# Merging the last two down groups and turning x through HBM ahead of the odd mixer

## The chip, the core and the metric

The kernel runs on one core of one Trainium2 chip. The core has a matrix engine (TensorE: PE in the profile, with its weight loads as PEld), a vector engine (VectorE, DVE), a scalar engine (ScalarE, ACT), GpSimd (POOL) and a sync engine (SyncE, SP) that only issues DMAs here. Each engine runs its own program in order, and the programs meet at semaphores. The metric is the device time of one execution in microseconds, lower is better.

## What is computed

Two layers over 256 tokens with 2048 features, all in float32. Each layer is a mixer and a gated convolution FFN, each behind an RMS norm, each added to x. Cut to what matters here:

```python
for i in range(2):
    h = rms_norm(x, norm_mix_g[i])
    if i == 0:   # "even" mixer: spatial gating and windowed pooling
        mix = concat([y_a, y_b]) @ w_out_even
    else:        # "odd" mixer: 16 heads of forgetting attention
        p = h @ w_in_odd          # q, k, v (2048 each) and 16 forget logits
        mix = forgetting_attention(q, k, v, cumsum(log_sigmoid(f + b))) @ w_out_odd
    x = x + mix
    up = rms_norm(x, norm_ffn_g[i]) @ w_up[i]              # 2048 -> 2 * 5632
    x = x + (silu(conv3(gate)) * conv3(val)) @ w_down[i]   # 5632 -> 2048
return rms_norm(x, final_norm_g)
```

## The kernel before

**Pieces.** All weights stream through in 369 pieces of 1 MB. SyncE loads a piece into one of four `raw` slots (`load`, L299), ScalarE rounds it to a high part (`high`, L457), VectorE subtracts to get the low part (`low`, L858), and TensorE multiplies: high weights with the high and the low part of the activations, low weights with the high part. The scalar and the vector program are written out piece by piece: at step k they do the piece that TensorE needs three pieces later (`LEAD = 3`), and other work is put at chosen steps around it. `high` of piece c+3 may begin when TensorE is through piece c-1, since the slot is a ring of four. `load` of a piece waits for the low part of the piece four before it.

**x and h.** x lies as `x[128 tokens, 2 tiles, 2048]`. The matrix products need h with features on partitions, `H[128, 16, 512]` (`h_split`: 256 columns high, 256 low). x is turned in four chunks of 512 features. A chunk is turned either by TensorE (`transpose_x`, 8 products with the identity, L1468) or by VectorE (`turn_blocks`, 16 transposes of 32 partitions, L902); then ScalarE multiplies with the norm's gain and rounds (`turned_high`, L495, four instructions), and VectorE forms the low part (`turned_low`, L882, four instructions). `s_turn` counts turned chunks, `s_turn_hi` their high halves, `s_turned` chunks of h that are ready; for the odd mixer (stage 2) they begin at 8, 16 and 8. The row scale of the norm (`rstd`) is applied later, to the outputs: ScalarE squares x (`squares`, L479), VectorE adds up (`mean_square`, L916), ScalarE takes the root (`root`, L502), VectorE refines it (`rstd_columns`, L921 to L925) and spreads it over a tile (`spread_rstd`, L941).

**The end of the first FFN.** The hidden features go in 11 groups. The last 16 pieces (`B + 116` on) are 8 of the last group's up projection, then 4 of the tenth group's down projection (`down(l, NG - 2)`) and 4 of the eleventh's. Each down piece gives 512 columns of x for one group: 24 products, then `add_to_x` (L911) adds them to x, 8 times in all. With the last four pieces TensorE also turns chunks 0, 1 and 2 of x. Steps 8 to 15 below are these eight pieces.

**The start of the odd mixer** (`heads_of_group(0)`, called M0 to M11 below, one per piece). M0 and M1 are the first half of the v projection, M2 and M3 first halves of q and k; before M4 TensorE does `forget_sums` (16 products, L1698), then the second half of v. VectorE turns chunk 3 in M0, ScalarE and VectorE finish chunk 3 of h at step M2, and VectorE spreads rstd at the end of its step M2. The forget logits pass through ScalarE and VectorE at step 5, then through HBM by GpSimd (`c_rows`) into the bias tile that the first head's logits need at M9.

Of the kernel before, what the change touches and what calls it, by code (L numbers as in the profile page):

```python
# [25 lines left out]
F32 = mybir.dt.float32  # L26
# [23 lines left out]
def build(nc, x_in, norm_mix_g, norm_ffn_g, final_norm_g, w_in_even, ln_v_g, ln_v_b, w_spatial,  # L50
          b_spatial, w_pool, pool_scale, w_out_even, w_in_odd, b_forget, w_out_odd, w_up, conv_w,
          conv_b, w_down, out, c_dram):
# [21 lines left out]
    N_END = N_FFN[1] + 12 * NG  # L74
    OUT0_ORDER = [(c, q) for c in range(4) for q in (2, 3, 0, 1)]
# [8 lines left out]
    A_OUT0, A_FFN, A_OUT1 = 0, [4, 4 + 4 * NG + 4], 4 + 4 * NG  # L84
# [6 lines left out]
    X_READY = [0, A_OUT0, A_FFN[0] + 4 * (NG - 1), A_OUT1, A_FFN[1] + 4 * (NG - 1)]  # L91
# [8 lines left out]
    OUT = out[0].rearrange("(t p) d -> p t d", p=P)  # L100

    with ExitStack() as ctx:
# [67 lines left out]
        xT = [work[:, c0:c0 + 1024].rearrange("p (k t) -> p k t", k=4) for c0 in (0, 1024, 2048, 4096)]  # L170
        scaled = raw[:, 0:2, :]
# [29 lines left out]
        s_turn = sem("x_turned")  # L201
        s_turn_hi = sem("turned_high")
# [75 lines left out]
        def turned_bank(s, n, kk):  # L278


            if s in (1, 3) or (s, n) in ((0, 3), (2, 3)):
                return xT[n if s else 0][:, kk, :]
            return psT[:, 2 * (n % 2) + kk // 2, TOK * (kk % 2):TOK * (kk % 2) + TOK]
# [9 lines left out]
        def _(sp):  # L293
# [43 lines left out]
            def load_ffn(l):  # L337
                B = N_FFN[l]

                def panels(c, g, pair, r=0):  # L340

                    for j, first in enumerate((0, FF)):
                        for k in range(2):
                            col = value(sp, at(512 * g + 256 * pair + first, 512, r))
                            load(c + 2 * j + k, W_UP[l][:, 8 * k:8 * k + 8, bass.ds(col, 256)], r)

                def down(c, g, r=0):
                    row = value(sp, at(4 * g, 4, r))
# [12 lines left out]
                panels(B + 120, NG - 1, 1)  # L361
                down(B + 124, NG - 2)
                down(B + 128, NG - 1)
# [73 lines left out]
        def _(a):  # L437
# [47 lines left out]
            def turned_high(s, n):  # L485
# [5 lines left out]
                for kk in range(4):  # L491
# [5 lines left out]
                    if kk % 2:  # L497
                        fenced(ins, s_turn_hi, 8 * s + 2 * n + kk // 2 + 1)

# [131 lines left out]
            def ffn(l):  # L631
# [40 lines left out]
                for k in range(16):  # L672
                    if k >= 14 and l == 0:
                        turned_high(s + 1, k - 14)
# [30 lines left out]
                    if l == 0 and k >= 13:  # L705
                        squares(s + 1, k - 13)
# [21 lines left out]
            def heads_of_group(first, r=0):  # L728

                c = N_MIX1 + 12 * first  # L730
                for k in range(12):
                    hh = 4 * first
                    if first == 0 and k == 0:
                        turned_high(2, 2)
                        squares(2, 3)
                    if first == 0 and k == 1:
                        root(2)
                    if first == 0 and k == 2:
                        turned_high(2, 3)
                    if first == 0 and k == 5:  # L740
# [97 lines left out]
        def _(ve):  # L838
# [53 lines left out]
            def turn_blocks(s, n, tokens):  # L892
# [10 lines left out]
                if 3 in tokens:  # L903
                    ins.then_inc(s_turn, 1)

# [218 lines left out]
            def ffn(l):  # L1124
# [48 lines left out]
                for k in range(16):  # L1173
                    if k >= 14 and l == 0:
                        turned_low(s + 1, k - 14)
                    low(c + k + LEAD)
                    if k == 0:
# [18 lines left out]
                    if k >= 8 and not (l == 1 and k >= 12):  # L1196
# [50 lines left out]
            def heads_of_group(first, r=0):  # L1247
                c, hh = N_MIX1 + 12 * first, 4 * first
                for k in range(12):
                    if first == 0 and k == 0:  # L1250
                        turned_low(2, 2)
                        turn_blocks(2, 3, (0, 1))
                        mean_square(2)
                        turn_blocks(2, 3, (2, 3))
                    if first == 0 and k == 1:
                        rstd_columns(2)
                    if first == 0 and k == 2:
                        turned_low(2, 3)
# [9 lines left out]
                    if first == 0 and k == 5:  # L1268
# [108 lines left out]
        def _(pe):  # L1377
# [218 lines left out]
            def down(l, g, c, r=0, frm=0, transposes=False):  # L1596

                if frm:
                    pe.wait_ge(s_actlo, 22 * l + 2 * g + 2)
                else:  # L1600
                    pe.wait_ge(s_actlo, at(22 * l + 2 * g + 2, 2, r))
                for n in range(4):
                    i = A_FFN[l] + 4 * g + n
                    pe.wait_ge(s_xadd, at(i - 1, 4, r))
                    straight_quad(c + n, n % 2, Y, 4 * frm, True, True, r)
                    if transposes and n >= 1:
                        transpose_x(2, n - 1)
# [34 lines left out]
            def ffn(l):  # L1642
# [15 lines left out]
                down(l, NG - 2, B + 124)  # L1658
                if l == 0:
                    down(l, NG - 1, B + 128, frm=1, transposes=True)  # L1660
                else:
                    last_down(B + 128)
# [41 lines left out]
            def heads_of_group(first, r=0):  # L1704
                c, hh = N_MIX1 + 12 * first, 4 * first
                for k in range(12):
                    if first == 0:
                        j, part = MIX1_FIRST[k]
                        pe.wait_ge(s_turned, 9 + min(k, 2) if k < 4 else 12)
                        if k == 0:  # L1710
                            pe.wait_ge(s_xadd, A_FFN[0] + 4 * NG - 1)
                        if k == 4:
# [67 lines left out]
```

## Time and profile before

| | |
|---|---|
| median of 3 runs | 2087.44 us (2087.23 to 2087.59) |
| the profiled execution | 2087.08 us; its span from first to last instruction 2085.4 us |
| busy | PE 2075.2 us, PEld 1792.2, DVE 1594.9, ACT 1054.0, POOL 26.3 |
| DMA | 397.17 MB, mean 190 GB/s |
| TensorE clock granted | 0.999 of full speed |

The time outside the span is 1.7 us. In the timelines each row is a merged run of instructions: start in us from the span's start, length in us, engine, line, operation, output and inputs, and in brackets the idle time before it. A merged row's length reaches to the end of its last instruction, and the pipelined engines begin the next instruction a little before that, so lengths of neighbours overlap; the difference of two starts is what an instruction really takes from its engine.

### The profile page before, as it was taken

How to read it: one execution, taken by the hardware profiler on the slowest of the kernel's cores; microseconds unless marked ns; L12 is line 12 of the kernel's file. 1: busy time of each engine (PE TensorE's matmuls, PEld its weight loads, DVE VectorE, ACT ScalarE, POOL GpSimd, SP SyncE). 2: the span in 40 equal slices, each digit the busy share in tenths (PEclk: the TensorE clock that was granted, in tenths of full speed). 3: DMA queues.
4: the chain of work that ended last, by engine and by line, in shares of the span. 5: the costliest groups of instructions: out<-in, count | busy, mean ns of one | idle time of the engine just before them, and what ended most of it. 6: DMA issues, size and time to landing. Idle time of an engine off the chain costs nothing.

```text
span 2085.4 us, 29751 instructions
## 1 busy us (share of the span) xinstructions
PE 2075.2 (100%) x10928; PEld 1792.2 (86%) x10928; DVE 1594.9 (76%) x2053; ACT 1054.0 (51%) x1102; POOL 26.3 (1%) x57
## 2 busy tenths in 40 slices
PE   9999999999999999999999999999999999999998
PEld 7888888888888888888888888888888888888887
DVE  7988886777677776778788788997776777767676
ACT  7654564445444544456454554465454445444454
POOL 0000000000000000000010000000000000000000
PEclk9999999999999999999999999999999999999999
DMA  8656565565555655655565565556555556556553
GB/s 280 220 167 207 180 209 188 192 194 185 192 190 183 206 187 181 197 189 165 187 213 158 190 209 178 173 183 215 194 185 190 193 182 206 183 181 198 184 190 113
DMA packets 317621, 397.17 MB, mean 190 GB/s; under 512 B 8661, under 2 KB 241405, under 8 KB 317437
## 3 DMA queue, kind: packets, MB, share of 16 engines
q1 hardware_dynamic: 313932, 391.40, 57.0%
q0 software_dynamic: 1056, 3.16, 0.7%
q10 hardware_dynamic: 2576, 1.85, 0.3%
q8 instruction: 36, 0.59, 0.1%
q14 instruction: 21, 0.16, 0.0%
HBM read 394.28 MB, written 2.11 MB: 190 GB/s over the span
## 4 chain that ended last, share of the span: by engine, by line
PE 93%; DVE 3%; ACT 1%; issue 1%; SPq 1%; DMA 1%; DVEq 0%; ACTq 0%
PE ps_turned L1399 36%; PE ps_straight L1438 33%; PE ps_turned L1408 19%; PE ps_straight L1399 1%; PE ps_turned L1438 1%; DVE w_low L858 1%; PE ps_straight L1408 1%; DMA w_raw<-in_w_in_even 1%; ACT w_high L457 1%; DVE work L985 0%; PE ps_straight L1678 0%; SPq L311 0%; DVE work L864 0%; PE ps_straight L1688 0%; DVE work L941 0%
## 5 line engine op out<-in xcount | busy, mean ns | idle before, releaser
L858 DVE TENSOR_TENSOR w_low<-w_raw,w_high 128x2048 fp32r<-128x2048 f32 x369 | 844.6, 2292 | 330.0 <-ACT w_high L457 297.6
L457 ACT ACTIVATE w_high<-w_raw 128x2048 fp32r<-128x2048 f32 x368 | 704.4, 1918 | 662.0 <-PE ps_straight L1438 282.4
L1399 PE MATMUL ps_turned<-h_split,w_high 128*128 128x512 f32 x3456 | 802.9, 390 | 0.0
L1399 PEld LDWEIGHTS ps_turned<-h_split,w_high 128*128 128x128 f32 x3456 | 643.7, 188 | 130.4
L1408 PEld LDWEIGHTS ps_turned<-h_split,w_low 128*128 128x128 f32 x3456 | 425.4, 192 | 6.3 <-DVE w_low L858 0.3
L1408 PE MATMUL ps_turned<-h_split,w_low 128*128 128x256 f32 x3456 | 429.2, 283 | 0.0
L1438 PE MATMUL ps_straight<-w_high,y_split 128*128 128x512 f32 x1792 | 425.4, 390 | 0.1
L1438 PEld LDWEIGHTS ps_straight<-w_high,y_split 128*128 128x128 f32 x1792 | 336.0, 188 | 69.9 <-issue 0.5
L1438 PE MATMUL ps_straight<-w_low,y_split 128*128 128x512 f32 x896 | 221.3, 389 | 0.0
L1438 PEld LDWEIGHTS ps_straight<-w_low,y_split 128*128 128x128 f32 x896 | 168.2, 188 | 34.9
L1105 DVE SCALAR_TENSOR_TENSOR work<-work,conv_columns 128x256 f32<-128x256 f32 x352 | 154.6, 480 | 11.0
L911 DVE TENSOR_TENSOR x<-x,ps_straight 128x512 f32<-128x512 f32 x182 | 116.8, 683 | 54.3 <-PE ps_straight L1438 53.6
L614 ACT ACTIVATE work<-work,conv_columns 128x256 f32<-128x256 f32 x176 | 95.6, 591 | 61.0 <-DVE work L868 60.9
L466 ACT ACTIVATE work<-ps_turned 128x512 f32<-128x512 f32 x108 | 64.6, 598 | 80.4 <-PE ps_turned L1399 66.7
L864 DVE TENSOR_TENSOR work<-ps_turned,work 128x512 f32<-128x512 f32 x108 | 74.5, 690 | 27.6 <-ACT work L466 24.8
L1438 PE MATMUL ps_straight<-w_high,h_split 128*128 128x512 f32 x368 | 89.5, 395 | 0.0
L1438 PEld LDWEIGHTS ps_straight<-w_high,h_split 128*128 128x128 f32 x368 | 68.4, 188 | 13.9
L1237 DVE STREAM_TRANSPOSE work<-work 32x96 f32<-32x96 f32 x256 | 69.1, 270 | 13.1 <-DVE small L1225 7.9
L868 DVE TENSOR_TENSOR work<-work,rstd_rows 128x512 f32<-128x512 f32 x103 | 71.3, 692 | 3.5
L902 DVE STREAM_TRANSPOSE work<-x 32x256 f32<-32x256 f32 x160 | 69.7, 436 | 2.5
L1438 PE MATMUL ps_straight<-w_low,h_split 128*128 128x512 f32 x184 | 45.5, 389 | 0.0
L1438 PEld LDWEIGHTS ps_straight<-w_low,h_split 128*128 128x128 f32 x184 | 34.5, 188 | 7.2
(204 smaller groups left out, 760.7 us busy)
## 6 DMA issues: line engine op xcount, KB each, us to landing
w_raw<-in_w_up SPq DMA_DIRECT2D x176, 1024.0 KB, 5.0
w_raw<-in_w_down SPq DMA_DIRECT2D x88, 1024.0 KB, 5.0
w_raw<-in_w_in_odd SPq DMA_DIRECT2D x48, 1024.0 KB, 5.4
w_raw<-in_w_in_even SPq DMA_DIRECT2D x23, 1024.0 KB, 6.0
w_raw<-in_w_out_even SPq DMA_DIRECT2D x16, 1024.0 KB, 5.0
w_raw<-in_w_out_odd SPq DMA_DIRECT2D x16, 1024.0 KB, 5.2
work<-c_rows POOLq DMA_DIRECT2D x8, 256.0 KB, 6.4
x<-in_x SPq DMA_DIRECT2D x3, 512.0 KB, 11.3
```

What stands on the lines that cost most here:

```text
L457: a.activation(wh[:, s, :], raw[:, s, :], ACT.Copy).then_inc(s_high, 1)
L614: ins = a.activation(cc[j % 2][:, m, :], up[:, m, 2:], ACT.Identity, scale=taps[:, l, 2, bass.ds(i, 1)], bias=taps[:, l, 3, bass.ds(i, 1)])
L858: ve.tensor_tensor(wl[:, s, :], raw[:, s, :], wh[:, s, :].bitcast(F32), ALU.subtract).then_inc(s_low, 1)
L864: fenced(ve.tensor_tensor(to, src, spare, ALU.add), s_added, at(q + 1, 4, r))
L868: return ve.tensor_tensor(ap, ap, factor.unsqueeze(1).to_broadcast([P, 2, TOK]), ALU.mult)
L902: ins = ve.transpose(dst, src)
L911: ins = ve.tensor_tensor(xc, xc, psA[:, 2 * (i % 2) + t, :] if sums is None else sums[:, t, :], ALU.add)
L1105: ins = ve.scalar_tensor_tensor(out=c[:, m, :], in0=up[:, m, 2 - back:TOK + 2 - back], scalar=taps[:, l, 2 - back, bass.ds(i, 1)], in1=c[: ...
L1237: ins = ve.transpose(dst, src)
L1399: ins = pe.matmul(ps[:, 2 * slot + m, :], hi[:, kk, P * m:P * m + P], acts[:, K, :], start=(K == 0 and not narrow_ran), stop=(K == KC - 1) ...
L1408: ins = pe.matmul(ps[:, 2 * slot + m, TOK:], lo[:, kk, P * m:P * m + P], acts[:, K, 0:TOK], start=(K == 0 and opens), stop=(K == KC - 1), ...
L1438: return pe.matmul(ps[:, 2 * slot + t, :], acts[:, k0 + kk, a0:a0 + P], weights[:, kk, :], start=begin, stop=end)
```

## The change

1. **Order of the last eight down pieces.** `LAST0` takes the two groups together: chunk 0 of group ten, 1, 2, then chunks 0, 1, 2 of group eleven, then chunk 3 of both. The sums of both groups stay in PSUM, chunk 2 in `ps_turned`, so x is added to four times instead of eight, and chunk 0 of x is final after step 11.
2. **TensorE's transposes and VectorE's 16-part ones go.** ScalarE stores each final chunk of x to HBM with four DMAs (`store_column`, at steps 12, 13, 14 and M0), SyncE fetches it back with its 32 by 32 blocks regrouped (`fetch_blocks`, four DMAs a chunk, between the loads of M3, M4, M5, M6 and M7), and VectorE turns within the blocks by one instruction over 128 partitions and 1024 columns (`turn_within_blocks`).
3. **Steps.** Chunks 0 and 1 are turned at step 15, chunk 0 ahead of `low` of M2 and chunk 1 behind it; chunk 2 at step M2, chunk 3 at step M4 (before: M2). `forget_sums` goes from before M4 to before M5, its logits from step 5 to 6.

```diff
+    LAST0 = [(0, 0), (0, 1), (0, 2), (1, 0), (1, 1), (1, 2), (0, 3), (1, 3)]
+    X_COLUMNS = x_dram.rearrange("n a t i c -> n i a t c")
+    X_BLOCKS = x_dram.rearrange("n a t i (k j b) -> n j a (t i k) b", k=4, j=4)
@@ SyncE
+            def fetch_blocks(n):
+                sp.wait_ge(s_column[n], 64)
+                if n >= 2:
+                    sp.wait_ge(s_turn, 4 * 2 + n - 1)
+                for j in range(4):
+                    sp.dma_start(blocks[n % 2][32 * j:32 * j + 32, :].rearrange("p (m b) -> p m b", b=32),
+                                 X_BLOCKS[n, j]).then_inc(s_blocks[n % 2], 16)
             for n, (j, k) in enumerate(MIX1_FIRST):
                 load(N_MIX1 + n, ...)
+                if 3 <= n < 7:
+                    fetch_blocks(n - 3)
@@ ScalarE
+            def store_column(n):
+                a.wait_ge(s_xadd, X_READY[2] + n + 1)
+                for i in range(4):
+                    a.dma_start(X_COLUMNS[n, i], x[32 * i:32 * i + 32, :, 512 * n:512 * n + 512])\
+                        .then_inc(s_column[n], 16)
-                    if k >= 14 and l == 0:
-                        turned_high(s + 1, k - 14)
+                    if k == 15 and l == 0:
+                        turned_high(2, 0)
                     high(c + k + LEAD)
-                    if l == 0 and k >= 13:
-                        squares(s + 1, k - 13)
+                    if l == 0 and 12 <= k < 15:
+                        store_column(k - 12)
+                        squares(2, k - 12)
@@ ScalarE, heads_of_group
                     if first == 0 and k == 0:
-                        turned_high(2, 2)
+                        turned_high(2, 1)
+                        store_column(3)
                         squares(2, 3)
                     if first == 0 and k == 1:
                         root(2)
-                    if first == 0 and k == 2:
-                        turned_high(2, 3)
-                    if first == 0 and k == 5:
+                    if first == 0 and k in (2, 4):
+                        turned_high(2, 1 + k // 2)
+                    if first == 0 and k == 6:
@@ VectorE
+            def turn_within_blocks(n):
+                ve.wait_ge(s_blocks[n % 2], 64 * (n // 2 + 1))
+                ve.transpose(xT[2 + n % 2].rearrange("p k (g a) -> p k g a", a=32),
+                             blocks[n % 2].rearrange("p (g k b) -> p k g b", g=8, k=4)).then_inc(s_turn, 1)
-                    if k >= 14 and l == 0:
-                        turned_low(s + 1, k - 14)
+                    if k == 15 and l == 0:
+                        turn_within_blocks(0)
+                        turned_low(2, 0)
                     low(c + k + LEAD)
+                    if k == 15 and l == 0:
+                        turn_within_blocks(1)
+                        add_to_x(X_READY[2] + 3, 3, c + k)
+                        turned_low(2, 1)
+                    if l == 0 and k in (11, 12, 13):
+                        add_to_x(X_READY[2] + k - 11, k - 11, c + k, sums=psT if k == 13 else None)
@@ VectorE, heads_of_group
                     if first == 0 and k == 0:
-                        turned_low(2, 2)
-                        turn_blocks(2, 3, (0, 1))
                         mean_square(2)
-                        turn_blocks(2, 3, (2, 3))
-                    if first == 0 and k == 2:
-                        turned_low(2, 3)
+                    if first == 0 and k in (2, 4):
+                        turn_within_blocks(1 + k // 2)
+                        turned_low(2, 1 + k // 2)
-                    if first == 0 and k == 5:
+                    if first == 0 and k == 6:
@@ TensorE
+            def last_two_down0(c):
+                pe.wait_ge(s_actlo, 2 * NG - 2)
+                for n, (second, q) in enumerate(LAST0):
+                    ...
+                    straight_quad(c + n, (0, 1, 0, 1)[q], Y, 4 * second, second == 0, second == 1,
+                                  ps=psT if q == 2 else psA)
-                        pe.wait_ge(s_turned, 9 + min(k, 2) if k < 4 else 12)
+                        pe.wait_ge(s_turned, (9, 10, 10, 10, 11, 12)[min(k, 5)])
-                        if k == 4:
+                        if k == 5:
                             forget_sums()
```

## Rows read from the trace of the kernel before

**Rows 1.** The page: busy time by engine, and the chain that ended last.

```profile
PE 2075.2 (100%) x10928; PEld 1792.2 (86%) x10928; DVE 1594.9 (76%) x2053; ACT 1054.0 (51%) x1102; POOL 26.3 (1%) x57
PE 93%; DVE 3%; ACT 1%; issue 1%; SPq 1%; DMA 1%; DVEq 0%; ACTq 0%
```

**Rows 2.** Timeline of TensorE, end of the first FFN and start of the mixer.

```profile
926.18 3.79 PE L1438 MATMUL ps_straight<-w_high,y_split 128*128 128x512 f32 x16
...
953.38 3.79 PE L1438 MATMUL ps_straight<-w_high,y_split 128*128 128x512 f32 x16
...
958.82 1.03 PE L1468 MATMUL ps_turned<-ident,x 128*128 128x128 f32 x8
...
972.29 3.89 PE L1438 MATMUL ps_straight<-w_high,h_split 128*128 128x512 f32 x16
...
983.27 3.79 PE L1399 MATMUL ps_turned<-h_split,w_high 128*128 128x512 f32 x16
...
994.38 3.85 PE L1698 MATMUL ps_straight<-h_split,wf_split 128*48 128x512 f32 x16
...
1003.52 3.79 PE L1438 MATMUL ps_straight<-w_high,h_split 128*128 128x512 f32 x16
```

**Rows 3.** Timeline of ScalarE in the same stretch.

```profile
953.63 1.92 ACT L457 ACTIVATE w_high<-w_raw 128x2048 fp32r<-128x2048 f32 x1 [3.52 <-PE ps_straight L1438]
955.46 0.61 ACT L479 ACTIVATE work<-x 128x512 f32<-128x512 f32 x1
...
974.37 0.63 ACT L479 ACTIVATE work<-x 128x512 f32<-128x512 f32 x1
...
975.88 1.92 ACT L457 ACTIVATE w_high<-w_raw 128x2048 fp32r<-128x2048 f32 x1
977.82 1.28 ACT L502 ACT_TABLE_LOAD   x1
979.28 0.20 ACT L502 ACTIVATE small<-small 128x2 f32<-128x2 f32 x1 [0.17 <-DVE small L917]
979.51 1.92 ACT L457 ACTIVATE w_high<-w_raw 128x2048 fp32r<-128x2048 f32 x1
982.90 1.86 ACT L495 ACTIVATE h_split<-work,feature_columns 128x256 fp32r<-128x256 f32 x4 [1.47 <-DVE work L902]
984.79 1.92 ACT L457 ACTIVATE w_high<-w_raw 128x2048 fp32r<-128x2048 f32 x1
```

**Rows 4.** Timeline of VectorE in the same stretch.

```profile
955.64 2.29 DVE L858 TENSOR_TENSOR w_low<-w_raw,w_high 128x2048 fp32r<-128x2048 f32 x1 [0.78 <-DVE x L911]
...
988.30 1.67 DVE L882 SCALAR_TENSOR_TENSOR h_split<-work,feature_columns,h_split 128x256 fp32r<-128x256 f32 x4
990.00 2.29 DVE L858 TENSOR_TENSOR w_low<-w_raw,w_high 128x2048 fp32r<-128x2048 f32 x1
992.21 3.98 DVE L941 STREAM_TRANSPOSE rstd_rows<-small 32x64 f32<-32x64 f32 x16
...
996.55 4.49 DVE L858 TENSOR_TENSOR w_low<-w_raw,w_high 128x2048 fp32r<-128x2048 f32 x2
```

**Rows 5.** Groups of VectorE's transposes (ns: min/median/max), two widths.

```profile
L902 DVE STREAM_TRANSPOSE work<-x x160: 425/436/442, 27.7 to 1363.0; 32x256 f32<-32x256 f32 x160
...
L941 DVE STREAM_TRANSPOSE rstd_rows<-small x64: 225/236/242, 53.2 to 1374.7; 32x64 f32<-32x64 f32 x64
```

**Rows 6.** ScalarE's stores of the result (ns), and landing times of the result's stores.

```profile
L817 ACTq DMA_DIRECT2D result<-w_raw x2: 360/361/362, 2074.0 to 2081.5; - x2
...
DMA to landing us min/median/max: 1.9/2.7/3.4
```

**Rows 7.** DMA packets, 893 to 899 us (64-byte ones, ACT's queue) and 948 to 954.

```profile
q10 hardware_dynamic: 2083, 0.13, 23.3%
...
q1 hardware_dynamic: 1099, 1.11, 63.4%
```

**Rows 8.** Timelines of GpSimd and VectorE: the bias tile's end, the first logits.

```profile
1018.61 2.33 POOL L428 TENSOR_TENSOR work<-work,causal 128x256 f32<-128x256 f32 x2 [5.47 <-DMA work<-c_rows]
...
1026.49 0.74 DVE L1215 SCALAR_TENSOR_TENSOR work<-ps_straight,small,work 128x128 f32<-128x128 f32 x2 [1.21 <-PE ps_straight L1678]
```

More of the change, by code:

```diff
@@ L51, in build @@
           b_spatial, w_pool, pool_scale, w_out_even, w_in_odd, b_forget, w_out_odd, w_up, conv_w,
-          conv_b, w_down, out, c_dram):
+          conv_b, w_down, out, c_dram, x_dram):
     D = x_in.shape[2]
@@ L170, in build @@
         xT = [work[:, c0:c0 + 1024].rearrange("p (k t) -> p k t", k=4) for c0 in (0, 1024, 2048, 4096)]
+        blocks = [work[:, c0:c0 + 1024] for c0 in (0, 1024)]
         scaled = raw[:, 0:2, :]
@@ L201, in build @@
         s_turn = sem("x_turned")
+        s_column = [sem(f"x_column_stored{i}") for i in range(4)]
+        s_blocks = [sem(f"x_blocks_landed{i}") for i in range(2)]
         s_turn_hi = sem("turned_high")
@@ L361, in load_ffn @@
                 panels(B + 120, NG - 1, 1)
-                down(B + 124, NG - 2)
-                down(B + 128, NG - 1)
+                if l == 0:
+                    for n, (second, q) in enumerate(LAST0):
+                        row = 4 * (NG - 2 + second)
+                        load(B + 124 + n, W_DOWN[l][:, row:row + 4, 512 * q:512 * q + 512])
+                else:
+                    down(B + 124, NG - 2)
+                    down(B + 128, NG - 1)
             load_ffn(0)
@@ L1195, in ffn @@
                         take_up(l, k // 2, g)
-                    if k >= 8 and not (l == 1 and k >= 12):
+                    if l == 0 and k in (11, 12, 13):
+                        add_to_x(X_READY[2] + k - 11, k - 11, c + k, sums=psT if k == 13 else None)
+                    if l == 1 and 8 <= k < 12:
                         add_to_x(A_FFN[l] + 4 * (NG - 2) + k - 8, k % 4, c + k)
@@ L1594, in panel, with down @@
                 turned_panel(c, j, H, r)
[L1596 to L1601, printed above, removed]
+            def down(l, g, c, r=0):
+                pe.wait_ge(s_actlo, at(22 * l + 2 * g + 2, 2, r))
                 for n in range(4):
@@ L1604, in down @@
                     pe.wait_ge(s_xadd, at(i - 1, 4, r))
-                    straight_quad(c + n, n % 2, Y, 4 * frm, True, True, r)
-                    if transposes and n >= 1:
-                        transpose_x(2, n - 1)
+                    straight_quad(c + n, n % 2, Y, 0, True, True, r)
+            def last_two_down0(c):
+                pe.wait_ge(s_actlo, 2 * NG - 2)
+                for n, (second, q) in enumerate(LAST0):
+                    if n == 0:
+                        pe.wait_ge(s_xadd, X_READY[2] - 1)
+                    if n == 1:
+                        pe.wait_ge(s_xadd, X_READY[2])
+                    if n == 2:
+                        pe.wait_ge(s_added, Q_FFN[0] + 4 * NG - 1)
+                    if n == 3:
+                        pe.wait_ge(s_actlo, 2 * NG)
+                    if n == 6:
+                        pe.wait_ge(s_xadd, X_READY[2] + 2)
+                    straight_quad(c + n, (0, 1, 0, 1)[q], Y, 4 * second, second == 0, second == 1,
+                                  ps=psT if q == 2 else psA)
             def last_down(c):
@@ L1657, in ffn @@
                     panel(l, NG - 1, j, B + 116 + 2 * j)
-                down(l, NG - 2, B + 124)
                 if l == 0:
-                    down(l, NG - 1, B + 128, frm=1, transposes=True)
+                    last_two_down0(B + 124)
                 else:
+                    down(l, NG - 2, B + 124)
                     last_down(B + 128)
```

13 lines of the change are left out of this document (8 added, 5 removed).

## The prediction

> **What bounds the kernel now.** I read the page first: TensorE is busy for 2075.2 of 2085.4 us and carries 93% of the chain that ended last, while VectorE and ScalarE have idle time [rows 1]. So only work that leaves TensorE can shorten the kernel, and only a wait that stops TensorE can lengthen it; time saved on VectorE is worth nothing by itself. Then I read TensorE's timeline where the change acts. Nothing interrupts it there: six down pieces begin at 926.18 and end at 958.82, 5.44 us each, and the transposes, the mixer's first pieces and the forget sums follow without idle time [rows 2]. Last I read ScalarE's and VectorE's timelines of that stretch, to lay the new programs out in time, and the DMA rows, since x now goes out and back.
>
> **TensorE loses its transposes.** The first mixer piece starts at 972.29. Eight down pieces of 5.44 us from 926.18 would end at 969.70, so the 24 transposes cost 2.59 us. The first mixer piece also takes 5.54 us before the next one (972.29, two pieces, then 983.27: 10.98 against 10.88), 0.10 more than two plain ones [rows 2]. That is 2.7 us that go, and it is all that can go: the number of products in the eight down pieces stays 24 each. 2.7 us is 0.13% of 2087; about 0.2% (4.2 us) is what a measurement of this kernel can tell from no change. Four adds fewer (8 instructions) and one transpose in place of 16 spare VectorE time, which hides behind TensorE anyway.
>
> **New schedule of TensorE if it never waits.** M0 969.70, M1 975.14, M2 980.58; M2 takes 5.54 and M3 5.57 (983.27 to 994.38 holds the two pieces, 11.11) [rows 2], so M4 starts at 991.69 and the forget sums at 997.13. M1 wants chunk 1 of h, the forget sums all four.
>
> **The prices on the two other engines**, each the difference of two starts. High: 1.83 (953.63 to 955.46). A high starts 0.25 after the piece that frees its slot (953.38, 953.63). The low part starts 2.01 after the start of its high and takes 2.21 (990.00 to 992.21). Squares of a chunk: 1.51 (974.37 to 975.88). Table load and root: 1.52 (977.82 to 979.51, less the 0.17 of waiting). The high half of a chunk of h from SBUF: 1.89 (982.90 to 984.79); its low half: 1.70 (988.30 to 990.00). Spreading rstd with the scaled copy: 4.34 (992.21 to 996.55) [rows 2 to 4]. The new transpose of 1024 columns has no row; transposes of 64 and 256 columns take 236 and 436 ns [rows 5], 1.04 ns a column, so 436 + 768 x 1.04 = 1.24 us, 1.28 with the gap to the next instruction. Its bounds: 1.07 (the slope alone) and 4.9 (four quarters of 32 partitions one after another). I take 1.28, since the rows are of the same operation and a line through them fits.
>
> A store's issue on ScalarE is 0.36 each [rows 6]; with a gap to the next I take 0.45, 1.8 us for a chunk; bounds 1.4 and 4. The three stores ahead of M0 lie behind a high with idle time after it. The fourth, in M0, comes right behind a fenced turned_high and stands in the chain below at full price.
>
> **The chain of ScalarE and VectorE, step by step.**
> - Step 14: high of M1 at 958.82 + 0.25 = 959.07, low at 961.08, done 963.29. Chunk 0 turned 964.57.
> - Step 15: high half of chunk 0 until 966.46, high of M2, low of M2 at 968.47, done 970.68; chunk 1 turned 971.96. Chunk 0 of h is ready near 967.3, before 969.70.
> - M0: high half of chunk 1 until 973.85; its low half ends about 0.9 later, at 974.7, against 975.14 at M1. That is a margin of 0.4. The stores of chunk 3 until 975.65, squares 977.16, high of M3 978.99.
> - M1: table and root 980.51; low of M4 at 982.52, done 984.73. (VectorE's low of M3 and rstd end near 982.4, just before.)
> - M2: chunk 2 turned 986.01, high half 987.90, high and low of M5 989.91 to 992.12, spread rstd until 996.46. Chunk 2 of h is ready at 988.8, before M4 at 991.69.
> - M3: low of M6, 2.21, done 998.67.
> - M4: chunk 3 turned 999.95, high half 1001.84, the second half of its low part, 0.85, ends at 1002.7.
>
> TensorE wants the fourth chunk at 997.13 and gets it at 1002.7: **a new stall of 5.6 us**. In the kernel before, this chunk's low half came ahead of spread rstd, ending at 990.00, 4.4 us before the forget sums [rows 2, 4]; the change moves it behind spread rstd (4.34) and another low part (2.21). The forget sums moved one piece later gives 5.4 back, and the store of chunk 3 in ScalarE's path (1.8) takes some of it.
>
> **The sum.** The forget sums take 3.68 (994.38 to the next piece); the second v piece behind them starts at 1002.7 + 3.7 = 1006.4 where it started at 1003.52 [rows 2]. So +2.9 us: 5.6 of stall less 2.7 of transposes. On the profiled execution, 2087.08 + 2.9 = 2090.0; the median of the runs lies 0.4 above it, so 2090.3.
>
> **x through HBM.** Stores of chunk 0 are issued by about 951.9 and land 2.7 later (1.9 to 3.4) [rows 6], at 954.6. The load of M3 goes out before, at 952.5, and SyncE then waits for the stores; the load of M4 is due only after the next low, at 957.9, so the wait holds nothing up. Behind it stand loads that are used some 20 us later. A fetch is 4096 packets of 128 bytes. 64-byte packets took 0.233 x 6 us x 16 / 2083 = 10.7 ns each, mostly 1 KB ones 0.634 x 6 x 16 / 1099 = 55 ns [rows 7]; on that line 128 bytes are 13.7 ns, 256 packets on each engine, 3.5 us. The load of M3 ends near 957.5, chunk 1's stores take 1.3 of the engines (512 KB at some 400 GB/s), so chunk 0 lands at 962.3, wanted at 963.3. Chunk 1: load of M4 2.6, fetch 3.5, stores 1.3, 969.7, wanted at 970.7. The margins are 1 us each. Chunks 2 and 3 have over 5. Bounds of a packet: 10.7 ns, which leaves the sum as it is, and 55 ns, 14 us a fetch.
>
> The packets read alternate blocks of 128 bytes out of 512, so half of them start 128 bytes past a multiple of 256. The Trainium skill, "DMA: Bandwidth & Descriptors", How a descriptor splits into AXI transactions, says that a read starts at the 256-byte boundary below and that the bytes fetched ahead still cost beats. By that half the packets would cost as 256-byte ones and the fetch an estimated 4.2 us, which uses up most of the two margins and adds under 1 us. No run here shows it yet.
>
> **The forget path.** The bias tile is ready at 1020.94, 26.6 us after the forget sums started [rows 2, 8]; the first logits waited for TensorE until 1026.49. Now the sums start at 1002.7, the tile is ready near 1029.3, and TensorE's first scores, four pieces after 1006.4 (5.44, 5.57, 5.54, 5.54), near 1028.9. The logits may slip by half a us; the turned probabilities are wanted only at the end of M11, so I charge nothing.
>
> **Rivals.**
> - *No stall at the forget sums* (0.08). VectorE would have to reach chunk 3 by 991.5, 5.6 earlier. Then only the 2.7 us stay: 2084.7. Against it: the order is written out, VectorE has no idle time after 989.9 in the sum, and no price is off by half.
> - *The fetches come late* (0.22), the slower side. The mechanism is the price of a 128-byte packet on the 16 engines. From about 17 ns on, chunk 0 holds back VectorE at step 15 and with it chunks 1 to 3, which all follow in the chain. At 27 ns a fetch is 7 us: chunk 0 at 965.8, 2.5 late; then 2.6 + 7.0 + 1.3, chunk 1 at 976.7 against 973.2, 3.5 late. +6.0 on the forecast: 2096.3. For it: SyncE's one queue carries weights and fetches in order. Against it: the 64-byte packets at 10.7 ns [rows 7]. The same page, Specifications, puts line rate at 512 bytes and more and says a read-modify-write happens below; that would be this rival, and the rows of 64-byte packets speak for a small price rather than a large one.
> - *The transpose or the stores cost more* (0.10). Transposes of chunks 1, 2 and 3 each stand in the chain; at 2.0 us each, and 0.8 for a store's issue, it is 3 x 0.75 + 1.4 = +3.7, 2094.0.
>
> **How the numbers follow.** The forecast with its own range, 2088.6 to 2091.8 (prices off by 0.15 each way in the chain, margins used up or not), has 0.60. Of it a tenth lies over 2091.6. Range for all: 2088.0 to 2096.5 leaves out no stall (0.08), the tail of the late fetches and something I don't see. Faster by over 0.2% (below 2083.3) isn't possible by what leaves TensorE: 0.01. Slower by over 0.2% (above 2091.6): 0.06 and nearly all of the two dearer rivals, 0.19 and 0.08, 0.33. Within: 0.66.
>
> **What would show it.** TensorE idle for some 5.6 us ahead of the forget sums at 997, released by VectorE's low half (L882), and nowhere else; M0 at 969.7. One transpose of 1.2 us four times; spread rstd and a low part between chunk 2's low half and chunk 3's transpose. Fetches landing at or before VectorE's transposes: VectorE waiting on them is the second rival. If TensorE never idles at the forget sums, the order of VectorE's program was misread and the forecast falls.

## The result

The changed kernel takes 2094.55 us (2093.99 to 2095.78, 6 runs) against 2087.34 (2086.64 to 2087.75, 6 runs): +7.2 us, a ratio of 1.0036 with the 95% interval 1.0026 to 1.0046. The time lies in the range of the forecast (2088.0 to 2096.5), but 4.25 above its likeliest value of 2090.3 and 2.75 above the narrower range (2088.6 to 2091.8) to which the forecast gave 0.60. It is slower by more than 0.2%, to which the forecast gave 0.33.

The page of the changed kernel, busy time by engine and the chain that ended last, where [rows 1] stood: TensorE is busy for 2075.0 us against 2075.2, although the transposes are gone (the low clock described below takes 1.25 of them back, and 0.7 more busy time lies ahead of the changed stretch), and the chain leaves it more often, 90% on PE against 93%.

```profile
PE 2075.0 (99%) x10904; PEld 1790.6 (86%) x10904; DVE 1588.3 (76%) x2033; ACT 1054.7 (50%) x1102; POOL 25.9 (1%) x57
...
PE 90%; DVE 6%; ACT 2%; issue 1%; DMA 1%; SPq 0%; ACTq 0%; DVEq 0%
```

TensorE's timeline of the changed kernel, where [rows 2] stood (a bracket gives the idle time before a row and who ended it):

```profile
926.54 3.79 PE L1482 MATMUL ps_straight<-w_high,y_split 128*128 128x512 f32 x16
...
970.06 3.79 PE L1482 MATMUL ps_straight<-w_high,h_split 128*128 128x512 f32 x16
...
976.31 3.93 PE L1482 MATMUL ps_straight<-w_high,h_split 128*128 128x512 f32 x16 [0.65 <-DVE h_split L915]
...
992.99 3.82 PE L1482 MATMUL ps_straight<-w_high,h_split 128*128 128x512 f32 x16
996.65 1.98 PE L1482 MATMUL ps_straight<-w_low,h_split 128*128 128x512 f32 x8
1005.15 5.10 PE L1754 MATMUL ps_straight<-h_split,wf_split 128*48 128x512 f32 x16 [6.53 <-DVE h_split L915]
1010.09 3.83 PE L1482 MATMUL ps_straight<-w_high,h_split 128*128 128x512 f32 x16
```

This execution was 0.36 us later than the one of before by the first down piece (926.54, 926.18), which the change doesn't touch; I take that off below. The profiled executions of all the kernels below lie there from 0.6 us earlier to 1.4 later than the one of before. M0 then starts at 969.70, to the digit where the forecast put it. TensorE waits 0.65 us at M1 and 6.53 at the forget sums, both for the low half of h (L915), and the forget sums take 4.94 us (1005.15 to 1010.09) where they took 3.68. The piece behind them starts at 1009.73 against 1003.52: +6.2. Another 0.4 us comes at 1434 in the second FFN, and 0.36 is the later start: 7.0, the difference of the spans (2092.4 and 2085.4).

VectorE's timeline shows what it did in TensorE's wait (compare [rows 4]):

```profile
964.04 1.24 DVE L942 STREAM_TRANSPOSE work<-work 128x1024 f32<-128x1024 f32 x1
...
972.13 1.25 DVE L942 STREAM_TRANSPOSE work<-work 128x1024 f32<-128x1024 f32 x1 [0.57 <-DMA work<-x_columns]
...
987.05 1.24 DVE L942 STREAM_TRANSPOSE work<-work 128x1024 f32<-128x1024 f32 x1
...
994.43 3.97 DVE L980 STREAM_TRANSPOSE rstd_rows<-small 32x64 f32<-32x64 f32 x16
...
998.77 2.29 DVE L891 TENSOR_TENSOR w_low<-w_raw,w_high 128x2048 fp32r<-128x2048 f32 x1
1000.98 1.24 DVE L942 STREAM_TRANSPOSE work<-work 128x1024 f32<-128x1024 f32 x1
1003.19 1.82 DVE L915 SCALAR_TENSOR_TENSOR h_split<-work,feature_columns,h_split 128x256 fp32r<-128x256 f32 x4 [0.97 <-ACT h_split L519]
```

From 994.43 to 1000.98 VectorE spreads rstd and forms the low part of M6, neither of which TensorE wants yet, and only then turns chunk 3, for which TensorE has waited since 998.4. ScalarE's timeline of M0, where [rows 3] stood, shows the other delay; behind it the group of the stores (issue in ns, landing in us), where [rows 6] stood:

```profile
973.41 1.86 ACT L519 ACTIVATE h_split<-work,feature_columns 128x256 fp32r<-128x256 f32 x4 [4.23 <-DVE work L942]
975.30 2.52 ACTq L528 DMA_DIRECT2D x_columns<-x  x4
977.86 0.63 ACT L503 ACTIVATE work<-x 128x512 f32<-128x512 f32 x1 [2.59 <-issue]
```

```profile
L528 ACTq DMA_DIRECT2D x_columns<-x x16: 557/618/880, 949.8 to 977.2; - x16
...
DMA to landing us min/median/max: 2.5/4.6/6.8
```

### The profile page after: what moved, and what is told of

It is laid out like the page before. It is cut to its first block, busy times and chain, and to the rows that moved or that the text cites. A ratio compares the mean times of both kernels' runs of the same rounds, so it can differ in the third digit from the quotient of the medians.

```text
span 2092.4 us, 29669 instructions
## 1 busy us (share of the span) xinstructions
PE 2075.0 (99%) x10904; PEld 1790.6 (86%) x10904; DVE 1588.3 (76%) x2033; ACT 1054.7 (50%) x1102; POOL 25.9 (1%) x57
## 4 chain that ended last, share of the span: by engine, by line
PE 90%; DVE 6%; ACT 2%; issue 1%; DMA 1%; SPq 0%; ACTq 0%; DVEq 0%
PE ps_turned L1443 35%; PE ps_straight L1482 31%; PE ps_turned L1452 19%; DVE w_low L891 2%; DVE work L935 1%; PE ps_straight L1443 1%; ACT w_high L481 1%; PE ps_turned L1482 1%; DVE work L1144 0%; PE ps_straight L1452 0%; ACT h_split L519 0%; DVE rstd_rows L980 0%; DVE work L897 0%; DMA w_raw<-in_w_in_even 0%; DVE x L950 0%
## 5 line engine op out<-in xcount | busy, mean ns | idle before, releaser
L1482 PE MATMUL ps_straight<-w_high,y_split 128*128 128x512 f32 x1760 | 417.7, 389 | 0.4 <-DVE x L950 0.4
L1482 PEld LDWEIGHTS ps_straight<-w_high,y_split 128*128 128x128 f32 x1760 | 330.1, 188 | 69.2 <-issue 0.8
L950 DVE TENSOR_TENSOR x<-x,ps_straight 128x512 f32<-128x512 f32 x172 | 110.3, 682 | 52.4 <-PE ps_straight L1482 51.8
L935 DVE STREAM_TRANSPOSE work<-x 32x256 f32<-32x256 f32 x144 | 62.8, 436 | 2.2
L519 ACT ACTIVATE h_split<-work,feature_columns 128x256 fp32r<-128x256 f32 x52 | 23.7, 504 | 46.9 <-DVE work L935 29.6
```

The costliest lines, as they stand in the source:

```text
L935: ins = ve.transpose(dst, src)
L950: ins = ve.tensor_tensor(xc, xc, psA[:, 2 * (i % 2) + t, :] if sums is None else sums[:, t, :], ALU.add)
L1482: return pe.matmul(ps[:, 2 * slot + t, :], acts[:, k0 + kk, a0:a0 + P], weights[:, kk, :], start=begin, stop=end)
```

## The experiments

The predictions of each are quoted as they stood before the run. A median in the text is that of the kernel's own runs; the kernel before was 2087.3 each time.

**Chunk 3 ahead of the spread.** The first question is whether the order of VectorE's program makes the stall.

```diff
-                    if first == 0 and k in (2, 4):
-                        turn_within_blocks(1 + k // 2)
-                        turned_low(2, 1 + k // 2)
+                    if first == 0 and k in (2, 3):
+                        turn_within_blocks(k)
+                        turned_low(2, k)
-                    if first == 0 and k == 2:
+                    if first == 0 and k == 3:
                         spread_rstd()
```

> The changed kernel, but chunk 3 of x is turned and its h formed at step M3 ahead of the low part of M6, and the spread of rstd stands behind it instead of at M2. Theory (the order of VectorE's program makes the stall at the forget sums): VectorE turns chunk 3 at 994.4 of the changed kernel's timeline instead of 1001.0 and its low half ends near 998.4, where TensorE gets there at 998.43. TensorE's wait of 6.5 us goes to under 0.5, the forget sums take 3.7 again instead of 4.94, and the total falls by 7 to 8 us against the changed kernel's 2094.5: 2086.5 to 2087.5. Rival (the trip through HBM makes the stall): chunk 3 lands late, VectorE waits for its DMAs and most of the 6.5 us stays: 2092 or more.

2090.45 us, ratio 1.0014 (1.0004 to 1.0023). The stall at the forget sums is gone and they take 3.69 us (TensorE's timeline of this kernel). But only 4.1 of the 7 to 8 us that I expected came out, because a new wait stands ahead of M8:

```profile
997.12 1.98 PE L1482 MATMUL ps_straight<-w_low,h_split 128*128 128x512 f32 x8
999.22 3.85 PE L1754 MATMUL ps_straight<-h_split,wf_split 128*48 128x512 f32 x16
1002.91 3.81 PE L1482 MATMUL ps_straight<-w_high,h_split 128*128 128x512 f32 x16
...
1021.91 5.36 PE L1443 MATMUL ps_turned<-h_split,w_high 128*128 128x512 f32 x16 [2.25 <-issue]
```

M8 writes the PSUM bank that VectorE frees with the first q panel, and VectorE came to that at 1021.13, since low parts, spread and forget logits kept it busy from 1000 with one wait of 3.3 us for ScalarE. Behind the wait the granted clock was 0.50 (1021.91 to 1024.00) and the piece's 16 wide products took 5.2 us instead of 3.7. So in the changed kernel the order makes the stall, and behind it VectorE has no slack. The profile doesn't name who ended the wait ahead of M8; that it was VectorE is read from the program and its timeline here, and borne out by the kernel with the forget logits a step earlier, below.

**Products in the stall.** Does the wait itself cost more than its length?

```diff
+                        if k == 5:
+                            pe.wait_ge(s_turned, 11)
+                            warm(28)
                         pe.wait_ge(s_turned, (9, 10, 10, 10, 11, 12)[min(k, 5)])
```

> The changed kernel with 28 products of the identity with ones (some 6 us) put on TensorE between M4 and the forget sums, into the unused bank 3; they do nothing but fill the wait. Theory (the forget sums took 4.94 instead of 3.68 because the granted clock was 0.69 in the wait and 0.73 in the sums): the clock stays at 1.00, the forget sums take 3.7, and the total falls by 1.2 us to 2093.3, with the sums' start unchanged. Rival (the sums are slow for a reason of their own, their load from the other engines): they still take 4.9 and the total stays within 0.3 us of 2094.5.

2093.28 us (2092.06 to 2093.96), 1.3 below the changed kernel. Both stretches of both kernels, by windows: the wait, then the forget sums (after the two numbers of the window: its length, busy time of PE, PEld, DVE, ACT and POOL, PE's granted clock, DMA share and GB/s). First the changed kernel, then the one with products:

```profile
998.40:1005.15 6.75, 0.22 (x1) 0.03 (x1) 5.50 (x8) 2.84 (x5) 0.00 (x0) 0.69 0.53 164
1005.15:1010.09 4.94, 4.93 (x16) 2.53 (x17) 3.96 (x2) 2.69 (x2) 0.00 (x0) 0.73 0.18 51
```

```profile
998.88:1005.57 6.69, 6.41 (x57) 6.25 (x56) 5.48 (x7) 2.84 (x5) 0.00 (x0) 1.00 0.53 158
1005.57:1009.28 3.71, 3.71 (x17) 2.03 (x17) 2.74 (x2) 2.69 (x2) 0.00 (x0) 1.00 0.19 64
```

Less the later start of this execution (0.67), the sums start at 1004.90 against 1004.79, and they take 3.71 us at full clock against 4.94 at a mean of 0.73. Windows inside the sums of the changed kernel show that this mean is a stretch at 1.2 GHz and the rest at 2.4:

```profile
1005.15:1007.85 2.70, 2.69 (x7) 1.32 (x8) 1.72 (x1) 2.69 (x2) 0.00 (x0) 0.51 0.19 65
1007.85:1010.09 2.24, 2.24 (x11) 1.20 (x10) 2.24 (x2) 0.00 (x0) 0.00 (x0) 1.00 0.17 33
```

The 1.2 us are the price of the clock. The Trainium skill, "TensorE: Matmul & The Clock Gate", Part 1, says that the array's clock is gated by how busy TensorE has been; these windows agree, with idle time in front of the low clock.

**The stores of chunk 3 behind a high part.**

```diff
                         turned_high(2, 1)
-                        store_column(3)
                         squares(2, 3)
                     ...
                     high(c + k + LEAD, r)
+                    if first == 0 and k == 0:
+                        store_column(3)
```

> The changed kernel, but in M0 the four stores of chunk 3 are issued behind the squares and the high part of M3 instead of ahead of the squares. The four issues took 2.52 us in which ScalarE computed nothing. Theory (they stand at full price in the chain to the forget sums): behind a running high of 1.92 they cost only the 0.6 that sticks out, so the forget sums start 1.9 us earlier and the total falls by 1.9 to 2092.6. Rival (the chain runs through VectorE there): the sums start at the same time and the total stays at 2094.5.

2093.21 us. The forget sums start at 1003.34, less this execution's start of 0.45, at 1002.89 against 1004.79: 1.9 earlier, as expected; TensorE's wait falls from 6.53 to 4.81. The median falls by 1.3, less than the 1.9 that I expected; the sums of the profiled execution took 4.93, so the clock took no less than before. The issues now run beside the high part (both rows begin at 976.68):

```profile
976.68 1.92 ACT L481 ACTIVATE w_high<-w_raw 128x2048 fp32r<-128x2048 f32 x1
976.68 2.77 ACTq L528 DMA_DIRECT2D x_columns<-x  x4
979.49 1.28 ACT L533 ACT_TABLE_LOAD   x1 [0.89 <-issue]
```

**Chunk 1 fetched ahead of the load of M4.**

```diff
+                if n == 4:
+                    fetch_blocks(1)
                 load(N_MIX1 + n, ...)
-                if 3 <= n < 7:
+                if n in (3, 5, 6):
                     fetch_blocks(n - 3)
```

> The changed kernel, but SyncE fetches chunk 1 ahead of the load of M4 instead of behind it. VectorE waited 0.57 us for chunk 1's landing at 972.13. Theory (the 1 MB load ahead of the fetch holds it back, by 2.6 us of transfer and by the queue's issue): chunk 1 lands some 4 us earlier, VectorE doesn't wait, TensorE's wait at M1 falls from 0.65 to near 0.1, and the total falls by 0.6 to 1.0. Rival (chunk 1's stores decide, which landed late): the wait on the DMA stays, and so does the time.

2094.61 us, no gain. The mechanism held: VectorE no longer waits for the fetch, M1 comes only 0.13 us later than without any wait (0.81 in the changed kernel), and the forget sums start 0.5 us earlier (1003.81, plus 0.48 for this execution's early start, is 1004.29). But they took 6.11 us, not 4.94, at a clock of 0.57:

```profile
997.00:1003.81 6.81, 0.10 (x1) 0.03 (x1) 5.57 (x8) 2.84 (x5) 0.00 (x0) 0.88 0.54 166
1003.81:1009.92 6.11, 6.11 (x16) 2.99 (x17) 4.49 (x2) 2.69 (x2) 0.00 (x0) 0.57 0.35 102
```

How much of the sums falls into the low clock differs from execution to execution of the same kernel, too: the changed kernel run again,

> The changed kernel as it is, on the same chip, for comparison: 2094.5, with TensorE waiting 6.5 us ahead of the forget sums.

took 2095.45 us (2094.61 to 2096.36), and its sums 6.39 us at 0.54. A gain of half a us ahead of such a wait can't be read from medians; I read it from the start of the sums.

**The order alone, in the kernel before.** x turned as before, with chunk 3 of h at M4 and the forget sums and logits a piece later.

```diff
-                    if first == 0 and k == 2:
+                    if first == 0 and k == 4:
                         turned_high(2, 3)      # ScalarE; turned_low(2, 3) the same on VectorE
-                    if first == 0 and k == 5:
+                    if first == 0 and k == 6:
-                        pe.wait_ge(s_turned, 9 + min(k, 2) if k < 4 else 12)
+                        pe.wait_ge(s_turned, (9, 10, 11, 11, 11, 12)[min(k, 5)])
-                        if k == 4:
+                        if k == 5:
                             forget_sums()
```

> The kernel before with part 3 of the change alone: the high and low half of chunk 3 of h at step M4 behind the spread of rstd and the low part of M6, the forget sums ahead of M5, their logits at step 6. x is turned as before, by TensorE and by VectorE's 16 transposes. Theory (the order stalls only because the new path makes ScalarE and VectorE late by then; before, VectorE would end chunk 3's low half near 998.8, and TensorE gets to the forget sums at 999.8): no wait, 2087.3 within 0.5. Rival (the order by itself costs the stall): TensorE waits 5 us or more and the total is 2092 or more.

2087.24 us, ratio 1.0000 (0.9991 to 1.0009). VectorE ends the low half of chunk 3 at 998.7 and TensorE starts the sums at 999.85 without a wait (VectorE's timeline, then TensorE's):

```profile
990.50 3.97 DVE L941 STREAM_TRANSPOSE rstd_rows<-small 32x64 f32<-32x64 f32 x16
...
997.05 1.67 DVE L882 SCALAR_TENSOR_TENSOR h_split<-work,feature_columns,h_split 128x256 fp32r<-128x256 f32 x4
...
999.85 3.88 PE L1698 MATMUL ps_straight<-h_split,wf_split 128*48 128x512 f32 x16
```

So the order by itself is free by a margin of 1.1 us. It stalls in the changed kernel because there the spread starts 3.6 us later (994.43 less 0.36 against 990.50) and the transpose and ScalarE's high half come behind it too, where before chunk 3 had long been turned, and because TensorE is 2.7 us earlier.

**Fetches made twice, and fetches in large packets.** These price the second rival.

```diff
                                  X_BLOCKS[n, j]).then_inc(s_blocks[n % 2], 16)
+                if n < 2:
+                    sp.wait_ge(s_blocks[n], 64)
+                    for j in range(4):
+                        sp.dma_start(..., X_BLOCKS[n, j]).then_inc(s_blocks[n], 16)
```

> The changed kernel with the fetches of chunks 0 and 1 made twice, one after the other. It prices late fetches, the second rival of the prediction. A second fetch of 4096 packets takes some 4.5 us to land. Theory (a fetch that lands later than VectorE gets to it moves the whole chain): VectorE waits some 4.5 us for chunk 0 and 3.5 to 4 more for chunk 1, TensorE waits at M0 and M1, and the forget sums start 7 to 9 us later; with the clock that falls in the waits 2102 to 2106. Rival (there is room before the forget sums that takes the delay up): under 2098.

2105.94 us, +11.4 on the changed kernel. VectorE waited 11.0 us in all for the two chunks, and TensorE 3.53 at M0, 4.58 at M1 and 3.76 at the forget sums. Those started at 1015.10, 10.3 later than in the changed kernel; I had expected 7 to 9. VectorE waited 10.4 more than in the changed kernel and the sums start 10.3 later: lateness of a fetch goes into their start one for one. The time of 2105.94 is within the expected 2102 to 2106.

From the DMAs' group, who waited for the fetches and the times:

```profile
  DVE work L947: 11.0, 2
```

In the other kernel each quarter of a chunk is fetched as 32 rows of 4 KB, so the x that is turned has its blocks in the wrong places:

```diff
-                    sp.dma_start(blocks[...].rearrange("p (m b) -> p m b", b=32), X_BLOCKS[n, j])
+                    sp.dma_start(blocks[...], X_ROWS[n][:, 1024 * j:1024 * j + 1024])
```

> The changed kernel with the same bytes fetched as rows of 4 KB in place of 128-byte blocks (128 packets a chunk's quarter at most, not 1024); the turned x is then not the right one, everything else is unchanged. Theory (the small packets cost about 3.6 us of all 16 DMA engines a chunk, where the bytes alone cost 1.3, and this made chunk 1 late): each fetch lands some 2 us or more earlier, VectorE's wait of 0.57 us for chunk 1 goes, TensorE's wait at M1 falls under 0.2, and the forget sums start 0.5 to 0.7 us earlier. Rival (ScalarE's stores land late and decide): the same wait remains.

VectorE's wait for chunk 1 is gone (for chunk 0 it waited 0.23), M1 comes 0.20 us late in place of 0.81, and the forget sums start 0.6 us earlier. The median, 2094.8, doesn't show it: the sums took 5.40 us at a mean clock of 0.65. So small packets cost the change 0.6 us, no more. It is the same wait that the earlier fetch takes away, so the two gains don't add up.

**Three moves together.** The first, third and fourth edit in one kernel.

> The changed kernel with three moves together: chunk 3 turned at M3 ahead of the low part of M6 with the spread of rstd behind it, the stores of chunk 3 issued behind the high part of M3, and chunk 1 fetched ahead of the load of M4. With the first move alone TensorE no longer waited at the forget sums but 2.4 us ahead of M8, for the PSUM bank that VectorE frees behind the forget logits (VectorE had no idle time from 1000 to 1027), and the clock fell to 0.50 there. Theory (what decides is how early ScalarE and VectorE are at M0; each us gained there takes a us off the last wait): the 1.9 us of the stores remove the rest of the wait, none of over 0.5 us is left in the mixer's start, the clock stays at 1.00, and the 2.7 us of the transposes come out less some 0.9: 2085.3 to 2086.5. Rival (VectorE is the bound there whatever its start): the wait ahead of M8 stays at 1.5 us or more, and the total at 2088.5 or more.

2087.20 us, ratio 0.9999 (0.9990 to 1.0008): the time of the kernel before. No wait that the profile lists is left at M1 or at the forget sums, the sums take 3.72, and the clock stays at 1.00, also behind the wait of 0.65 us that stayed ahead of M8:

```profile
1018.01 3.88 PE L1446 MATMUL ps_turned<-h_split,w_high 128*128 128x512 f32 x16 [0.65 <-issue]
```

0.8 us more came in small delays between the first scores and 1079, so my 2085.3 to 2086.5 was missed by 0.7. Both theories were half right: the two moves that were added shortened the wait ahead of M8 from 2.25 to 0.65 (which share is the stores' and which the fetch's, this run doesn't separate), and VectorE still was the bound behind it.

**The forget logits a step earlier.** On top of that:

```diff
-                    if first == 0 and k == 6:
+                    if first == 0 and k == 5:
                         ve.wait_ge(s_fT, 2)
                         ...
+                    low(c + k + LEAD, r)
+                    if first == 0 and k == 5:
                         ve.wait_ge(s_fe, 1)
                         ...                    # scan; the low part stood behind it
-                    low(c + k + LEAD, r)
```

On ScalarE the two copies of the logits stand ahead of the high part of M8, the exponential and the logarithm behind it.

> The three moves together, and the forget logits a step earlier: VectorE's sums of the logits stand ahead of the low part of M8, its scan behind it, and ScalarE's exponential and logarithm behind the high part of M8, so that VectorE does the low part in the 3.3 us in which it waited for them. Theory (VectorE has no slack from the forget sums to the first heads, and the time before M8 is given to that wait): the scan ends some 2.2 us earlier, the 0.65 ahead of M8 and most of the 0.7 us of small waits in the first heads go, and the total falls by 0.8 to 1.5 against the 2087.2 of the three moves: 2085.7 to 2086.4, the first version below the kernel before. Rival (the small waits come from the heads' own order): only the 0.65 goes, 2086.6 or more.

2085.69 us (2084.51 to 2086.81, 11 runs), ratio 0.9991 (0.9982 to 1.0000), as expected. VectorE goes from the logits through the low part into the scan without a wait:

```profile
1008.86 0.28 DVE L1325 TENSOR_SCALAR work<-work 16x256 f32<-16x256 f32 x1
1009.18 2.29 DVE L895 TENSOR_TENSOR w_low<-w_raw,w_high 128x2048 fp32r<-128x2048 f32 x1
1011.39 0.67 DVE L1329 TENSOR_TENSOR_SCAN work<-work 16x256 f32<-16x256 f32 x1
```

TensorE runs through the whole start of the mixer, and the piece behind the forget sums comes 2.6 us earlier than before, counted from the down pieces (1002.32 less 1.40, against 1003.52): all but 0.1 of what the forecast let go with the transposes. The medians are only 1.6 apart: 0.4 is lost at 1434 (below), and the rest I did not trace. The interval of the ratio ends at 1.0000, at the edge of no change.

**The stores of chunk 3 by GpSimd.** On top of that again, `store_column(3)` on GpSimd.

> The kernel with the forget logits earlier, and the stores of chunk 3 issued by GpSimd in place of ScalarE; GpSimd is idle there. Theory (the 0.6 us of issue that stick out behind the high part of M3 still stand in the chain): the low half of chunk 3 ends 0.6 earlier, which only matters if TensorE still waits for ScalarE or VectorE somewhere in the mixer's start: 0 to 0.6 us less. Rival (GpSimd's stores land later than ScalarE's and chunk 3 comes late): VectorE waits for the fetch of chunk 3, and the total is above that of the kernel with the forget logits earlier.

2085.61 us, ratio 0.9994 (0.9985 to 1.0003): the same. The low half of chunk 3 begins 0.8 us earlier than in the kernel with the forget logits earlier (992.90 less 0.09, against 995.00 less 1.40), and VectorE doesn't wait for the fetch. TensorE waited for neither engine there any more, so this buys nothing.

## Why the prediction held, and where it didn't

**What the forecast had right.** That 2.7 us leave TensorE and no more: M0 at 969.70, and 2.6 in the kernels without stalls. The transposes at 1.24 us, from a line through two widths [rows 5]: 1.24. The stall, its place and its cause: low half of chunk 3, behind the spread and a low part; the first experiment removed it by that order, and the order alone in the kernel before shows that the lateness of the new path belongs to the cause. The forget path through HBM and GpSimd held nothing up in the changed kernel.

**What was luck.** With the mechanism right, the size was off by more than the forecast's narrower range allowed. The time fell into the range for all only because that range reached up to 2096.5 for late fetches, and late fetches made 0.6 of the 4.25 us that were missing. That the whole range held is luck in part.

**Store issue, 1.8 us for a chunk.** This term was mis-sized: 2.51 to 3.02. I took 0.36 from the stores of the result [rows 6]; these take 0.62 at the median. It cost 0.4 at step 14 (stores and squares of chunk 1 reached into the time of M1's high part: 959.47 against 959.07) and 0.8 at M0. My statement that the first three stores lie behind idle time was wrong for that one. The third experiment shows that the M0 stores stand in the chain: moving them gave back 1.9 of their 2.56 us (975.30 to 977.86), of which the forecast had 1.8.

**Chunk 1 landed late by 0.6.** I gave it a margin of 1.0. It landed at 971.8 (972.13 less 0.36) where the forecast had 969.7, 2.1 later, and VectorE, itself 0.4 late, waited 0.6 for it. So TensorE waited at M1 too, where the forecast had it wait nowhere but at the forget sums. Its packets were priced well: alone, chunk 3's fetch ran from 985.4 to 988.9 with 4107 packets at 105.4% of 16 engines, 14.4 ns each, against the estimate of 13.7. The Trainium skill, "DMA: Bandwidth & Descriptors", How a descriptor splits into AXI transactions, says that a read starts at the 256-byte boundary below its first byte; the forecast's estimate from that was 4.2 us a fetch, and these 3.5 us are nearer to the line through the rows. What I had missed is the queue: SyncE's issue of the four fetches of a chunk, which has no price in the forecast, took 5.2 to 6.2 us for chunks 0 to 2 (up to 3.6 for one) and 2.8 for chunk 3, and the next load's issue 2.6 against 0.37 before. With 4 KB rows the four issues took 1.7 to 2.1. The load of M4 went out at 959.2 (959.59 less 0.36) where the forecast had 957.9. How much of the 2.1 us is issue and how much transfer, no run separates. SyncE's timeline, and the group of the fetches:

```profile
954.35 5.19 SPq L398 DMA_DIRECT2D work<-x_columns  x4
959.59 2.62 SPq L307 DMA_DIRECT2D w_raw<-in_w_in_odd  x1
```

```profile
L398 SPq DMA_DIRECT2D work<-x_columns x16: 544/737/3575, 954.3 to 986.1; - x16
```

Together the two terms and 0.3 of small gaps put the forget sums at 1004.79 where the forecast had 1002.7.

**The clock.** The forecast took the forget sums at 3.7 us and named no price for waiting beside its length. That is the step that failed: they took 4.94, and 6.39 in another execution. The products in the stall show it: with them the sums take 3.71, and the median is 2093.3 in place of 2094.55.

**The sum again.** 5.6 of stall less 2.7 was +2.9. Measured: +2.1 in the chain, +1.25 by the clock, 6.2 at the mixer; +0.4 at 1434. On the forecast's 2090.3 this gives 2094.05; the median lies 0.5 above, and the profiled execution (2094.26) was one of the quicker ones. The 0.4 at 1434 is in every kernel with the trip through HBM and not in the kernel with the order alone: TensorE waits 0.41 us for an add to x in the first loop of the second FFN. In the kernel before, too, the piece begins 0.13 us behind the end of the add (1427.45, 1427.58), 0.2 later than right behind the piece ahead of it, so the add was at the edge there already. What makes VectorE 0.35 later at that point I did not find.

**The rivals.** Late fetches were the right kind of mechanism with a small size: 0.6 us of them came true, and the fetches made twice show that each us counts. The dearer stores came true at half the price that I gave. No stall at all did not happen. Where I said that nothing waits once the stall is gone, I was wrong by one engine: VectorE's next debt falls due at M8. That didn't touch the forecast, but it hid half of the gain from the first repair.

## What to carry to other kernels

When work leaves the engine that bounds the kernel, lay out the programs of the others from that point in start-to-start times before placing the moved steps: the engine comes earlier by what it lost, and every step on the way to its next operand must come earlier too. Here waits of the matrix engine of 2.25 us and more cost their length and then some at half clock, while waits of 0.65 to 0.8 us left the clock at 1.00; so a stall of some us is worth more than its length. DMA issues are instructions of the engine that makes them: put them behind a long one that is already running.

## What the runs showed of the hardware

- Waits of 6.5 to 6.8 us on TensorE were followed by forget sums at a mean granted clock of 0.73, 0.57 and 0.54 (the changed kernel, the one with the early fetch, the changed kernel again): 4.94, 6.11 and 6.39 us for the same 16 products that take 3.7 at 2.4 GHz. A wait of 2.25 us had 2.1 us at 0.50 behind it (chunk 3 ahead of the spread); waits of 0.65 us at M1 (the changed kernel) and ahead of M8 (three moves together) had a clock of 1.00 behind them.
- Four DMAs of 64 rows of 2 KB from 32 partitions took ScalarE 0.62 us each to issue; one of 128 partitions took 0.36. During the four of chunk 3 the high part that was already running went on, and the next instruction began only behind them (976.68 and 979.49, the stores behind a high part).
- A DMA of 1024 packets of 128 bytes took SyncE 0.55 to 3.6 us to issue, the most for the third of four (chunks 0 to 2; for chunk 3 all four took 0.55 to 0.73). 64-byte, 128-byte and, for the most part, 1 KB packets cost 10.7, 14.4 and 55 ns of an engine in the windows read.
